# Memory keys computed one head at a time in the gaps ahead of up0, ml_in, up1 and up2

## The reference, cut to what matters

```python
def memory_attention(q_m, mem, mem_norm, w_kv, q_norm, k_norm):
    B, S, _ = q_m.shape
    q = rmsnorm(q_m.reshape(B, S, MEM_HEADS, MEM_HEAD_DIM), q_norm)
    kv = rmsnorm(mem, mem_norm) @ w_kv
    M = mem.shape[1]
    k = rmsnorm(kv[..., :MEM_WIDTH].reshape(B, M, MEM_HEADS, MEM_HEAD_DIM), k_norm)
    v = kv[..., MEM_WIDTH:].reshape(B, M, MEM_HEADS, MEM_HEAD_DIM)
    ...
```

## Time and profile before

| | before |
|---|---|
| median of 3 runs | 1652.88 us (1652.65 to 1653.32) |
| span of the profiled execution | 1642.0 us |
| median less that span | 10.9 us |
| TensorE products, busy | 1577.3 us, 96% |
| TensorE weight loads, busy | 1496.1 us, 91% |
| VectorE busy | 1062.7 us, 65% |
| ScalarE busy | 799.3 us, 49% |
| GpSimd busy | 382.8 us, 23% |
| moved by DMA | 252.19 MB, mean 154 GB/s |

### The profile page before, as it was taken

One profiled execution on the slowest core, in us unless ns is written; L12 is line 12 of the kernel. 1 busy time (PEld: TensorE's weight loads), 2 busy tenths in 40 slices (PEclk: granted clock), 3 DMA queues, 4 the chain that ended last, 5 costly groups with the idle time before them and its releaser, 6 DMA issues.

```text
span 1642.0 us, 33837 instructions
## 1 busy us (share of the span) xinstructions
PE 1577.3 (96%) x14025; PEld 1496.1 (91%) x14025; DVE 1062.7 (65%) x1531; ACT 799.3 (49%) x1202; POOL 382.8 (23%) x384
## 2 busy tenths in 40 slices
PE   6999999899999999999999999999999898899998
PEld 6898998789899998978999999999996798899998
DVE  6785565473888737566888476665565765666653
ACT  7773333554555546545555453444533246364432
POOL 0014442003166420012465326220000000212210
PEclk9998999999999999999999999999999999999999
DMA  7462220344355454622554565545623532545543
GB/s 273 148 207 79 54 55 3 148 164 156 126 179 171 147 184 152 208 77 84 188 184 145 188 203 190 203 139 195 225 103 129 206 124 95 192 158 201 184 163 113
DMA packets 42508, 252.19 MB, mean 154 GB/s; under 512 B 5616, under 2 KB 7776, under 8 KB 20384
## 3 DMA queue, kind: packets, MB, share of 16 engines
q1 hardware_dynamic: 38416, 233.20, 41.7%
q0 software_dynamic: 3984, 17.46, 3.8%
HBM read 249.47 MB, written 1.17 MB: 153 GB/s over the span
## 4 chain that ended last, share of the span: by engine, by line
PE 78%; DVE 8%; issue 7%; ACT 5%; DMA 2%; POOL 0%; SPq 0%; ACTq 0%; DVEq 0%; POOLq 0%
PE bank L424 22%; PE bank L425 21%; PE bank L426 21%; PE bank L1248 3%; DVE w_lo L297 2%; ACT w_hi L294 1%; DVE rs L579 1%; DMA sq<-rows_scratch_q 1%; ACT work L2451 1%; PE bank L626 1%; PE bank L442 1%; DVE mix L585 1%; PE bank L1418 0%; PE bank L443 0%; PE bank L444 0%
## 5 line engine op out<-in xcount | busy, mean ns | idle before, releaser
L424 PE MATMUL bank<-work_r,w_hi 128*128 128x256 f32 (+2 forms) x3248 | 926.4, 285 | 17.2 <-DVE w_lo L297 7.9
L425 PE MATMUL bank<-work_r,w_hi 128*128 128x256 f32 (+2 forms) x3248 | 918.9, 283 | 0.0
L426 PE MATMUL bank<-work_r,w_lo 128*128 128x256 f32 (+2 forms) x3248 | 918.1, 283 | 0.0
L297 DVE TENSOR_TENSOR w_lo<-ring,w_hi 128x2048 fp32r<-128x2048 f32 (+2 forms) x233 | 497.4, 2135 | 324.0 <-ACT w_hi L294 323.9
L424 PEld LDWEIGHTS bank<-work_r,w_hi 128*128 128x128 f32 x3248 | 616.6, 190 | 30.6 <-DVE w_lo L297 12.7
L294 ACT ACTIVATE w_hi<-ring 128x2048 fp32r<-128x2048 f32 (+2 forms) x233 | 408.4, 1753 | 463.2 <-PE bank L426 463.1
L426 PEld LDWEIGHTS bank<-work_r,w_lo 128*128 128x128 f32 x3248 | 616.7, 190 | 0.0
L425 PEld LDWEIGHTS bank<-work_r,w_hi 128*128 128x128 f32 x3248 | 615.9, 190 | 0.3
L1631 POOL TENSOR_TENSOR work<-work 128x272 f32<-128x272 f32 (+1 forms) x44 | 92.7, 2108 | 136.7 <-ACT work L1593 136.7
L535 POOL TENSOR_TENSOR sq<-sq 128x256 f32<-128x256 f32 (+2 forms) x36 | 57.5, 1599 | 250.2 <-ACT sq L513 249.4
L1619 DVE SCALAR_TENSOR_TENSOR work<-work,params_sb 128x272 f32<-128x272 f32 (+1 forms) x176 | 99.1, 604 | 5.2 <-DVE work L1619 0.3
(11 more groups left out here) (449 smaller groups left out, 1744.6 us busy)
## 6 DMA issues: line engine op xcount, KB each, us to landing
ring<-in_stream SPq DMA_DIRECT2D x166, 1024.0 KB, 4.9
ring<-in_stream SPq DMA_DIRECT2D x64, 704.0 KB, 4.1
ring<-in_stream SPq DMA_DIRECT2D x10, 768.0 KB, 4.3
work<-rows_scratch POOLq DMA_DIRECT2D x12, 512.0 KB, 5.5
work<-rows_scratch POOLq DMA_DIRECT2D x4, 544.0 KB, 6.2
work<-rows_scratch_o POOLq DMA_DIRECT2D x1, 2176.0 KB, 8.9
ring<-in_stream SPq DMA_DIRECT2D x3, 512.0 KB, 7.2
work<-rows_scratch_m POOLq DMA_DIRECT2D x1, 1088.0 KB, 7.4
```

Source lines behind the costliest of these rows:

```text
L297: eng.tensor_tensor(w_lo[:, slot, 0:size], raw_w, w_hi[:, slot, 0:size].bitcast(F32), ALU.subtract).then_inc(lo_done, 1)
L424: pe.matmul(out, w_hi[:, slot, at:at + P], hi, start=first, stop=False)
L425: pe.matmul(out, w_hi[:, slot, at:at + P], lo, start=False, stop=False)
L426: mm = pe.matmul(out, w_lo[:, slot, at:at + P], hi, start=False, stop=last)
```

## The change

The phase `mem_k` (two slabs of two products) becomes four phases `mem_k0` to `mem_k3` of one slab of one product, half a slab of weights each. They stand ahead of up0, ml_gates, up1 and up2. TensorE runs `mem_key_pe` where it ran `idle_products`; ScalarE copies each head's keys (`mem_key_act`), behind the fourth input of the gap, or, ahead of ml_in, behind the eighth.

For this the memory is fetched when the gates of the first layer are done, squared by GpSimd during gdn_out, summed by TensorE ahead of its slab 5, and normed by VectorE behind its products 5 and 6. ScalarE stores the normed memory to a scratch in DRAM before it reads product 7. GpSimd fetches it back three times: for head 1, for heads 2 and 3, and into `memn` for the values. `kmem` moves to the columns of the constant `level`, which is widened by 128 columns.

In the projections, in_qm follows in_ckv directly. The ckv sums move behind in_qm, the cq norm of VectorE into the middle of in_qm, the rotation's sine of ScalarE behind the row root. The weights are stored as before, and SyncE reads half of each row of a stored slab. The mLSTM's banks follow the new count of products.

```diff
-    ("in_uv", 4, 2, 1, 16, True), ("in_cq_kr", 2, 2, 1, 16, True), ("in_ckv", 1, 2, 1, 16, True), ("mem_k", 2, 2, 1, 16, False),
+    ("mem_k3", 1, 1, 1, 8, False), ("up2", 22, 2, 1, 16, True), ("down2", 16, 1, 2, 11, True),
+    ("in_uv", 4, 2, 1, 16, True), ("in_cq_kr", 2, 2, 1, 16, True), ("in_ckv", 1, 2, 1, 16, True),
...
             def body(un):
+                if name == "gdn_out" and un.j == 5:
+                    norm_act(act, 0, None, 8, SEQ, D, kind="mem", table=False)
+                if name == "gdn_out" and un.j == 7:
+                    act.wait_ge(*S.at("mem_dve", "k7"))
+                    act.dma_start(scr_mem.rearrange("p (a b) -> p a b", b=SEQ), mem0).then_inc(S.sem("mem_out"), 16)
                 un.ready(act)
                 square(act, un.j, un.bank()[:, 0:n], n)
...
         def mem_pool(pool):
-            pool.wait_ge(*S.at("norm_add", 7, 3))
-            pool.dma_start(memn, mem_t.rearrange("(k p) t -> p k t", p=P)).then_inc(S.sem("mem_in"), 16)
+            pool.wait_ge(*S.at("gate_dve", turn=15 + 4))
+            pool.dma_start(mem0, mem_t.rearrange("(k p) t -> p k t", p=P)).then_inc(S.sem("mem_in"), 16)
...
+        def mem_fetch(pool, dst):
+            pool.dma_start(dst, scr_mem.rearrange("p (a b) -> p a b", b=SEQ)).then_inc(S.sem("mem_back"), 16)
+
+        def mem_norm_dve(dve, slab):
+            if slab == 5:
+                S.begin("mem_dve")
+                dve.wait_ge(*S.at("mem_act", "rms"))
+                S.inc(dve.reciprocal(rs[:, 0, 0:SEQ], rs[:, 1, 0:SEQ]), "mem_dve", "rstd")
+                S.own(dve, "mem_dve")
+            for k in {5: range(3), 6: range(3, DB)}.get(slab, ()):
+                S.inc(dve.scalar_tensor_tensor(out=mem0[:, k, :], in0=mem0[:, k, :], scalar=pm("mem_norm", k), in1=rs[:, 0, 0:SEQ],
+                                               op0=ALU.mult, op1=ALU.mult), "mem_dve", f"k{k}")
+
+        def mem_key_pe(pe, h):
+
+            if h == 0:
+                pe.wait_ge(*S.at("mem_dve", "k7"))
+            else:
+                pe.wait_ge(S.sem("mem_back"), 16 * min(h, 2))
+            src = mem0 if h == 0 else mem_kept
+            stream_pe(pe, MEM_KEYS[h], lambda m, k: src[:, k, :], SEQ)
...
+        def mem_key_act(act, h):
+            un = Unit(PLAN[MEM_KEYS[h]], 1, 0, 0, 0)
+            un.ready(act)
+            un.free(act.activation(kmem[:, h, :], un.bank()[:, 0:SEQ], ACT.Copy))
...
@@ gpsimd
             gate_pool(pool)
+            mem_pool(pool)
             square_sums_pool(pool, 0, "norm", 1, T)
+            phase_read(pool, "gdn_out")
+            pool.wait_ge(S.sem("mem_out"), 16)
+            mem_fetch(pool, mem_kept)
             conv_up_pool(pool, 0)
...
             ml_gate_pool(pool)
+            pool.wait_ge(*S.at("ml_pe", "num3"))
+            mem_fetch(pool, mem_kept)
...
-            mem_pool(pool)
+            pool.wait_ge(*S.at("norm_add", 7, 3))
+            mem_fetch(pool, memn)
...
@@ scalar
                 for k in range(DB):
                     act.wait_ge(*S.at("norm_add", k, 2 * layer))
                     input_act(act, k, gain("norm_w", (4 * layer + 2) * DB), MIXED[layer])
+                    if k == 3:
+                        mem_key_act(act, 2 * layer)
...
             up_act(act, "up2")
-            norm_act(act, 0, None, 8, SEQ, D, kind="mem")
+            act.preload_act_table(ACT.Sqrt)
...
-            mem_k_act(act, (0, 1))
             norm_act(act, 0, None, 3, SEQ, 384, kind="cq", table=False)
+            each_product(act, "in_qm", 1, nothing, turns=0, split="hi")
             norm_act(act, 0, None, 2, SEQ, 256, kind="ckv", table=False)
             sg_root_act(act)
-            mem_k_act(act, (2, 3))
-            act.preload_act_table(ACT.Sin)
-            rope_act(act)
-            act.preload_act_table(ACT.Sqrt)
...
             rown_act(act, 2, [], SEQ, 8, 1.0 / P, cn("eps"), table=False)
+            act.preload_act_table(ACT.Sin)
+            rope_act(act)
+            act.preload_act_table(ACT.Sqrt)
...
@@ vector
-            each_product(dve, "gdn_out", 1, nothing, turns=0, split="lo", end="hold")
+            each_product(dve, "gdn_out", 1, lambda un: mem_norm_dve(dve, un.j), turns=0, split="lo", end="hold")
...
             third_slab(dve, "lo", "down2")
-            norm_dve(dve, 0, SEQ, lambda k: memn[:, k, :], gain("mem_norm"), lambda k: memn[:, k, :], 8, kind="mem")
...
@@ tensor
+            stream_pe(pe, "gdn_out", split_input(pe, O_HI, O_LO, T, by_step(pe, 2, per=2)), T,
+                      between=lambda slab: mem_norm_pe(pe) if slab == 5 else None)
...
-                idle_products(pe)
+                mem_key_pe(pe, 2 * layer)
...
-            mem_norm_pe(pe)
...
-            pe.wait_ge(*S.at("mem_dve", "k7", 0))
...
-            stream_pe(pe, "mem_k", lambda m, k: memn[:, k, :], SEQ, between=latent_sums)
-            stream_pe(pe, "in_qm", in_x, SEQ)
+            stream_pe(pe, "in_qm", in_x, SEQ, between=latent_sums)
+            norm_pe(pe, 0, 2, SEQ, kind="ckv")
```

More of the change, by code:

```diff
@@ L79 @@
 CROSSED = ("down0", "down1", "down2")
+MEM_KEYS = [f"mem_k{h}" for h in range(MEM_H)]
 def part_of(ph, j):
@@ L106, in plan @@
     for name in STORED:
+        if name == "mem_k":
+            for h in range(MEM_H):
+                out[f"mem_k{h}"].word0 = word + h // 2 * 2 * DB * P * P
+            word += MEM_H * DB * P * P
+            continue
         ph = out[name]
@@ L2089, in program, with project_dve @@
         mem_rows = area(gate_at, 8, SEQ)
-        def project_dve(dve, name, dst):
+        def project_dve(dve, name, dst, between=None):
             each_product(dve, name, 1, lambda un: (
-                un.ready(dve), un.free(dve.tensor_tensor(dst(un.j), un.bank()[:, 0:SEQ], scale2, ALU.mult))), turns=0, split="lo")
+                un.ready(dve), un.free(dve.tensor_tensor(dst(un.j), un.bank()[:, 0:SEQ], scale2, ALU.mult))), turns=0, split="lo", between=between)
         def uv_act(act):
@@ L2783, in _ @@
             rope_dve(dve)
-            project_dve(dve, "in_qm", lambda j: qmT[:, j, :])
             sg_weights_dve(dve)
@@ L2831, in gates_block @@
                 pe.wait_ge(*S.at("x_lo", k, 4))
-            def idle_products(pe):
-                for i in range(8):
-                    pe.matmul(ps[6][:, 0:T], ones, cn("causal"), start=True, stop=True)
             first_norm_pe(pe)
```

50 lines of the change are left out of this document (28 added, 22 removed).

## The result

| | before | after |
|---|---|---|
| median, us | 1652.11 (6 runs, 1648.40 to 1653.32) | 1635.03 (6 runs, 1625.85 to 1639.65) |
| profiled execution: span, us | 1642.0 | 1624.0 |
| the same execution's time, us | not listed | 1625.85 |

A forecast was written before the change was run, and what follows sets the result against it. TensorE, busy for 96% of the span, was taken to bound the kernel. Terms of -12.0, -3.6, +0.9 and 0 summed to -14.7 us, so 1652.88 became 1638.2 us, with a range of 1634.0 to 1645.5.

The forecast's parts named there:

- part 2: Seam of up2 and down2: memory norm leaves, removing TensorE's wait and the clock's fall; -3.6 us, between -4.1 and -2.
- part 3: gdn_out: multiplies and store delay the square of product 7, GpSimd's sum may add; +0.9 us, bounds +0.4 and +1.5.
- part 1: Projections: memory keys leave, saving 13.6 us, with a new 1.6 us wait in mla_q; -12.0 us, between -13.9 and -7.
- The frame: Whole kernel: 10.9 us between the profiled span of 1642.0 and the median of 1652.88 taken as unchanged.
- The bound below: Projections: -13.9 us if mla_q has no wait and in_qm runs faster without the rotation's arithmetic on VectorE beside it.
- rival B: Projections: the key products' cover was worth more, so only -7 us there, 1643.2 us in total; chance 0.12.
- what stays for the residual's chain: Down2's start: a wait for the first residual's chain, 4.2 us against a slab of 3.95, leaves 0.3 us.
- the lock rule: gdn_out: VectorE with two SBUF inputs and GpSimd share a lock, the loser fully blocks; +1.5 us, total 1638.8.
- rival C: gdn_out: GpSimd's fifteen operations at 2.60 us each hold TensorE at slab 5; 1656.0 us in total; chance 0.03.
- Part 4: Four gaps: key products replace unused ones, TensorE idles 1.5 to 1.8 us; 0 us, between -0.2 and +1.8.
- Rival A: Gaps and mla_q's wait: clock falls where TensorE idles longer, 1.7 us a time, up to 1646.7 us; chance 0.15.
- Rival D: Gaps: key products come late for a fetch, slab or bank; 4 us in three gaps gives 1650.2 us; chance 0.03.

The follow-up runs named there:

- seam_out: Kernel before without the memory norm's reciprocal and eight multiplies at the start of down2, memory used unnormalised; 1644.77 us, ratio 0.9987.
- experiment 4: Changed kernel with ScalarE's memory store behind product 7's square and copy, and four mla_q reads ahead of the row squares; 1634.70 us, ratio 0.9904.
- change_again: The changed kernel run again with no edit, for a second trace; 1637.00 us, ratio 0.9922.
- change_third: The changed kernel run again with no edit, for a third trace; 1631.82 us.
- experiment 9: Kernel before with six unused products instead of eight in each of the four gaps; 1650.33 us.
- the filled seam: Kernel before with four unused products ahead of down2's slab 3, where TensorE waits for VectorE; 1652.46 us.

## Why the prediction was right

It said 1638.2, the median is 1635.0, and the sum of the parts was -14.7 against -14.2 to -14.4 by the ledger. The agreement of the sum is better than that of its terms: part 2 gave 0.5 us less than forecast, part 3 cost 0.3 more and part 1 gave 0.3 more, each within its bounds; that they nearly cancel is luck. The 3.2 us between 1638.2 and 1635.0 are mostly the starting point: 1652.88 lies 4.5 us above the mean of the 41 executions of the kernel before.

**The frame was wrong, the difference not.** "10.9 us lie outside the span" is false: in every execution with both numbers the time is the span plus 1.8 or 1.9 us (1625.85 and 1624.0). The profiled execution of the kernel before was one of the shorter ones, at some 1643.9. Since all terms were differences, the error fell out, but the first step should have been to doubt an overhead of 10.9.

**Part 1** (-12.0 forecast, -12.3 measured). The keys' 13.62 us went as worked out, and another 0.4 beside them: the two slabs of in_qm took 5.44 and 5.85 us (1195.03 to 1200.47, 1203.30 to 1209.15), 0.2 less than the 11.49 before, and the variance 1.53 instead of 1.73. The bound below had named such a gain and put it down to the sine's arithmetic, which no longer runs beside in_qm; no run takes that alone, so the reason is not shown. mla_q's start moved by 14.03 us against the last split of the projections. The chain behind it was predicted at 6.9 us from the end of ckv's sums to TensorE's resumption and took 6.82 (1210.01 to 1216.83), the wait 1.48 where 1.6 was said; it costs 1.72, as its removal shows. The sine's table loads behind the row root were priced at nothing: ScalarE finished the key squares at 1234.65, and TensorE wanted them at 1246.41. So rival B had no ground: that cover was 11.8 us deep.

**Part 2** (-3.6 forecast, -3.1 in the mean). The mechanism was right, wait and clock both, and the sizes inside it were off in both directions. The clock's share was 1.5 instead of 1.7, and the wait of 2.16 us was worth 2.4. The mis-sized term is what stays for the residual's chain: 0.41 to 0.56 us of waiting and 0.8 in the stretch, where 0.3 was said. -2.4 - 1.5 + 0.8 = -3.1. That the start of up2 got no credit was right: seam_out kept GpSimd there and was as fast.

**Part 3** (+0.9 forecast, +1.17 measured, within its bounds). All of it is the order on ScalarE, since experiment 4 gets all of it back: the multiplies end 0.94 us behind L551's start, where by the price of 0.41 each they would have ended 0.5 us earlier, and the issue with its hand-overs takes 0.43. The multiplies took 2.58 / 5 = 0.52 us each, the first two beside the end of GpSimd's sum (405.92 to 408.52), against 1.28 / 3 = 0.43 for the three in the slab before. By the lock rule of the Trainium skill ("SBUF — State Buffer", Who interferes with whom) the whole part would have been +1.5; the trace lies between that and the 0.9. GpSimd's fifteen operations ended at 385.03 with the sum's product at 390.85, a margin of 5.8 where 4 was worked out; rival C (1.5 us an operation) was far off, the measured price is 16.2 / 15 = 1.08.

**Part 4** (0 forecast, 0 measured). TensorE idled 1.46 to 1.58 us, the low end of 1.5 to 1.8, and the clock stayed at 1.00. Rival A's premise, a fall at 1.6 to 1.8, was not met. Its price was wrong too: 1.7 a gap was taken from the seam, where TensorE's pace sets the end; in a gap VectorE's does, and a fall at 2.20 us cost nothing, one at 3.12 us 1.0 together with its longer idle time. Rival D didn't happen.

## What to carry to other kernels

Here a filler that only kept TensorE's clock up could be replaced by real products of nearly the same length at no cost, and what left the dense stage was gained but for what it had covered (12.3 of 13.6 us). When work is moved into a stage, look at each in-order engine for what its waits and DMA issues now stand ahead of: both new waits (worth 1.2 and 1.7 us) were orders on ScalarE, and swapping them cost nothing. Where executions differ by 1%, compare the same landmarks in several traces of each kernel, not two spans, and compare the stages without an edit too: two traces each would not have told chance from the 0.8 us at the row sums.

## What the runs showed of the hardware

TensorE's stream of split products has two paces at the same granted clock of 1.00. Windows of the first trace of the change and of change_again, in up2, with no wait in either:

```profile
1000.00:1020.00 20.00, 20.00 (x179) 20.00 (x178) 13.88 (x14) 7.13 (x9) 3.98 (x7) 1.00 0.54 187
```
```profile
1000.00:1020.00 20.00, 20.00 (x172) 20.00 (x172) 12.94 (x14) 8.07 (x8) 4.57 (x8) 1.00 0.56 202
```

179 against 172 matmuls in 20 us, one pace kept for the whole stage (103.42 or 107.48 us for up2, 97.98 or 101.82 for up3, where kernels with and without the change were slow). What sets the pace is open. With the fall of the clock in the first layer's mixer and at the branches, these are most of what the traces of one kernel differ by; for the executions without a trace it is not shown.

Around 2.2 us, idle time of one length did or did not lower the clock, and always did at the seam (five traces of five, 2.16 us; the sixth had the filler). Behind 2.16 us there it was at 0.50 to 0.56, and 2.29 us of idle time in a gap left it at 1.00. Two other places, near the start of the program and at the branches, have waits of varying length. At the first the clock fell behind 2.25 to 2.44 us (five traces) and not behind 1.28 to 2.11 (six). At the second it fell behind 1.93, 2.00, 2.12 and 2.22 us and not behind 1.38 to 1.74 (four). TensorE's timeline and the window behind the shortest of these, from change_third:

```profile
1383.69 0.36 PE L432 MATMUL bank<-work_r,w_hi 128*128 128x256 f32 x1 [1.93 <-DVE w_lo L305]
```
```profile
1384.70:1387.90 3.20, 3.20 (x17) 3.20 (x16) 2.25 (x2) 0.00 (x0) 2.36 (x2) 0.50 0.70 248
```

So the gaps of the change (up to 1.58 us) had less room than the 2.2 us of experiment 9 suggest. The Trainium skill ("TensorE: Matmul & The Clock Gate", What's actually happening) says that activity releases a throttle which is otherwise on; that fits the falls, but that sentence alone doesn't sort these cases, and what does is open. A wait also doesn't cost just its idle time: the 1.48 us in mla_q cost 1.72 and the slab that came 2.16 us late at the filled seam 2.43, while the 1.20 us at the end of gdn_out cost 1.17.
